# Sharing out projection chunks unevenly over the 32 attention items

## The reference, cut to what matters

```
proj = x @ w_in                       # queries, keys, values of four branches, and 4 x 1024 gates
y_c = moba_attention(...)             # "C": softmax
y_d = stick_breaking_attention(...)   # "D": see below
y_b = swa_sink_attention(...)         # "B": softmax in a window
y_a = dsa_attention(...)              # "A": softmax over the best 128 keys of an index score

# D, for each block of 128 queries:
z = q k^T * scale
log_keep  = where(strict, log_sigmoid(-z), 0)
log_after = reverse_cumsum(log_keep) - log_keep
a = where(strict, exp(log_sigmoid(z) + log_after), 0);  y = a v
```

## Time and profile before

| | |
|---|---|
| median of 3 runs | 1699.27 us (1697.19 to 1700.87) |
| the profiled execution | 1699.09 us, span 1697.4 us |
| PE busy | 1676.4 us (99% of the span) |
| DVE / ACT / POOL busy | 1225.5 / 779.0 / 818.4 us |
| granted TensorE clock, mean | 0.996 |
| the 32 items | from about 69 us to about 311 us |

### The profile page before, as it was taken

The page is one execution under the profiler, slowest core; times in us unless marked ns, Lnnn a source line. Parts: engine busy times, 40 slices in busy tenths (PEclk is TensorE's granted clock), DMA queues, the critical chain, the costliest instruction groups (busy, mean ns, idle before and its releaser), DMA issues.

```text
span 1697.4 us, 24495 instructions
## 1 busy us (share of the span) xinstructions
PE 1676.4 (99%) x9013; PEld 1483.0 (87%) x9013; DVE 1225.5 (72%) x2490; ACT 779.0 (46%) x1318; POOL 818.4 (48%) x493
## 2 busy tenths in 40 slices
PE   9999999999999999999999999999999999999997
PEld 7777777788889999999999999999888888888886
DVE  3588995512173985979988888435988888888886
ACT  4545545522334444773676477433333333333332
POOL 6332232444551667776866777775433233323312
PEclk9999999999999999999999999999999999999999
DMA  5121122243331566997899799997999999999952
GB/s 204 63 75 50 50 80 70 87 144 101 127 112 38 180 215 192 376 379 254 290 382 368 228 319 370 385 381 282 406 392 352 368 394 344 380 380 348 386 198 87
DMA packets 126502, 417.63 MB, mean 246 GB/s; under 512 B 12976, under 2 KB 32432, under 8 KB 124848
## 3 DMA queue, kind: packets, MB, share of 16 engines
q1 hardware_dynamic: 70320, 232.81, 39.1%
q0 software_dynamic: 36864, 134.23, 21.0%
q10 hardware_dynamic: 19200, 49.03, 7.3%
HBM read 364.91 MB, written 50.86 MB: 245 GB/s over the span
## 4 chain that ended last, share of the span: by engine, by line
PE 93%; DVE 3%; DMA 1%; POOL 1%; ACT 1%; issue 1%; SPq 0%; ACTq 0%; another core or an unknown queue 0%; DVEq 0%
PE ps L1365 18%; PE ps L1366 18%; PE ps L1367 17%; PE ps L1624 10%; PE ps L1627 10%; PE ps L1625 10%; PE ps L1735 5%; PE ps L1477 1%; PE ps L1429 1%; POOL w_lo L459 1%; PE ps L1460 1%; DMA raw<-w_units 1%; DMA x_raw<-xT 0%; PE ps L1406 0%; PE ps L1426 0%
## 5 line engine op out<-in xcount | busy, mean ns | idle before, releaser
L1365 PE MATMUL ps<-tok_hi,w_hi 128*128 128x384 f32 (+1 forms) x1472 | 526.4, 358 | 4.3 <-issue 4.3
L560 ACT ACTIVATE w_hi<-raw 128x1024 fp32r<-128x1024 f32 x330 | 348.9, 1058 | 389.3 <-PE ps L1627 291.3
L1367 PE MATMUL ps<-tok_hi,w_lo 128*128 128x384 f32 (+1 forms) x1472 | 517.4, 351 | 0.0
L1366 PE MATMUL ps<-tok_lo,w_hi 128*128 128x384 f32 (+1 forms) x1472 | 517.3, 351 | 0.0
L503 POOL TENSOR_TENSOR w_lo<-raw,w_hi 128x1024 fp32r<-128x1024 f32 x128 | 319.0, 2495 | 163.1 <-ACT w_hi L560 162.5
L459 POOL TENSOR_TENSOR w_lo<-raw,w_hi 128x1024 fp32r<-128x1024 f32 x76 | 183.4, 2416 | 319.7 <-ACT w_hi L560 319.5
L1365 PEld LDWEIGHTS ps<-tok_hi,w_hi 128*128 128x128 f32 x1472 | 276.7, 188 | 34.9 <-issue 15.2
L520 POOL DMA_INDIRECT v_got<-v_rows,eid x128 | 154.4, 1206 | 299.6 <-DVE own L1149 282.1
L1624 PE MATMUL ps<-w_hi,gh_hi 128*128 128x512 f32 x760 | 295.7, 389 | 0.0
L1625 PE MATMUL ps<-w_lo,gh_hi 128*128 128x512 f32 x760 | 295.7, 389 | 0.0
L1367 PEld LDWEIGHTS ps<-tok_hi,w_lo 128*128 128x128 f32 x1472 | 276.6, 188 | 18.1
(11 more groups left out here) (248 smaller groups left out, 1971.1 us busy)
## 6 DMA issues: line engine op xcount, KB each, us to landing
raw<-u_units SPq DMA_DIRECT2D x128, 512.0 KB
raw<-v_rows SPq DMA_DIRECT2D x128, 512.0 KB
raw<-w_units SPq DMA_DIRECT2D x78, 512.0 KB
gate_d<-stage ACTq DMA_DIRECT2D x12, 2048.0 KB
gelu_d<-gelu_t ACTq DMA_DIRECT2D x120, 192.0 KB
gelu_in<-gelu_d SPq DMA_DIRECT2D x30, 768.0 KB
gate_in<-gate_d SPq DMA_DIRECT2D x28, 768.0 KB
gate_in<-gate_d SPq DMA_DIRECT2D x2, 1536.0 KB
```

The source lines that it names most:

```text
L560: act.activation(hi_of(n), raw[:, n % RAW, :], ACT.Copy).then_inc(hi_done, 1)
L1365: pe.matmul(out_, l_hi, r_hi, start=start, stop=False)
L1366: pe.matmul(out_, l_hi, r_lo, start=False, stop=False)
L1367: return pe.matmul(out_, l_lo, r_hi, start=False, stop=stop)
```

## The change

Items 8 to 15 get shares of four, all others shares of three, in place of equal shares. The number of chunks in all (224) stays.

```
+D_SHARE, OTHER_SHARE = 4, 3
 ...
 def filled_by(s):
-    return 4 if s < -1 else KC + (KC * N_FILL - KC) * (s + 1) // N_ITEM
+    if s < -1:
+        return 4
+    shares = sum(D_SHARE if 8 <= i < 16 else OTHER_SHARE for i in range(s + 1))
+    return KC + (KC * N_FILL - KC) * shares // (8 * D_SHARE + 24 * OTHER_SHARE)
```

## The result

The changed kernel takes 1702.43 us in the median of 21 runs (1700.05 to 1708.87); the kernel before takes 1698.81 in 21 runs beside it (1697.19 to 1701.16). The ratio is 1.0022, 95% interval 1.0016 to 1.0028: 3.6 us slower; 1702.8 was forecast. The profiled execution took 1701.94, its span is 1700.2, its mean granted clock 0.997. In the changed file every line stands four lower: L1365 is now L1369, L1395 is L1399, L1426 is L1430, L572 is L576, L951 is L955.

The account below looks back on a forecast made before the run. PE, busy 99% of the span, was taken as the bound, so only its waits and clock count. Waits +2.1 and clock +1.45 on the profiled 1699.09, plus 0.18 to the median, gave 1702.8 us; range 1698.5 to 1706.

Parts of the forecast that it names:

- Item 6: Before unit 15, PE waits 3.55 us for ACT's value copy, which stands behind the exponentials of item 7 and one split.
- Item 7: Before unit 16, PE waits 0.9 us for ACT's value copy.
- Item 11: Before the weights, PE's present wait of 1.76 us for DVE's late `keep_lo` goes.
- Item 13: Before unit 22, PE waits 3.9 us for the value copy in place of 4.22; the covering chunks stand behind it.
- Items 14 and 15: Two POOL low parts in a row hold up DVE by up to 2.1 us more; extra chunks cover it, cost nothing.
- Item 24: In the B items PE closes in on DVE and waits 0.3 us for probabilities; bounds 0 and 1.5.
- Clock: Slow clock after the gap of item 6 costs 1.75 us; after item 13's it costs 2.05, 0.3 less than before.
- Sum: Over the whole kernel, waits of 8.65 less 6.57 give +2.1 us, clock +1.45, together +3.55: forecast 1702.8 us.
- 1 (the clock holds in item 6): All waits as forecast, but the 3.4 us gap in item 6 brings no slow clock: 1701.1 us; chance 24%.
- 2 (chunks cover item 13): PE reaches unit 22 no earlier than the copy, so that gap and its slow stretch go: 1696.5 us; chance 7%.
- 3 (DVE the bound in B): DVE becomes the bound in B and late D (items 14, 15, 24), adding 3.3 us: 1706.1 us; chance 12%.
- 4 (a shorter gap in item 6): ACT is free earlier, the gap in item 6 is shorter, nothing is felt: 1697.5 us; chance 4%.

Follow-up runs that it names:

- the run with the early copy: Changed kernel (four to three shares) with ACT's value copy moved ahead of the next item's exponents: 1695.02 us, ratio to before 0.9975.
- four to three shares and late low parts: Changed kernel with POOL held back in items 8 to 14 so low parts start later, value copy where it was: 1702.14 us, ratio 1.0013.
- equal shares with late low parts: Kernel before with POOL's low parts held back in items 8 to 14: 1691.59 us; with the value copy also moved ahead of the next item's exponents: 1690.68.
- the first items' shares alone: Kernel before with five chunks moved from items 0 to 7 into items 8 to 12, later items at 7: 1701.92 us, ratio 1.0013.
- the boundaries kept: Changed kernel, but items 0 to 6 keep 7 chunks and item 7 gets 2: 1700.33 us, ratio 1.0005.
- the gap filled: Changed kernel with 14 matmuls of unused result put into PE's gap in item 6: 1701.23 us, ratio 1.0012.
- equal shares with early copy: Kernel before (7 chunks an item) with ACT's value copy moved ahead of the next item's exponents: 1699.1 us, ratio 1.0.

## Why the prediction was right, step by step

- *Item 6*: right. 3.55 forecast, 3.58 measured, shown as 3.41. The copy that ends 0.1 ahead is the releaser, as the run with the early copy shows.
- *Item 7*: right. 0.9 forecast, 0.78 measured.
- *Item 11*: right. The 1.76 went.
- *Item 13*: the size came out, the reason only in part. I said 3.9, from a chain that is late by itself, "the same work when it arrives". Measured were 1.2 in item 12, which I had not named (the transposes of unit 20 wait for its read-out, behind the late chain), and 2.8 in item 13. The 2.8 are the floor above: the scores come later in PE's order, with two chunks between them and the boundary where there were five. I had used that very rule for item 6 and not asked it here. That 1.2 and 2.8 add up to about the 3.9 is luck. Before, the floor made only 0.3 of the wait (167.96 + 5.17 against 172.81, where PE was due), and the chain made the other 3.9 of the 4.22. The scores of the kernel before:

```profile
167.96 0.94 PE L1426 MATMUL ps<-projT 64*128 64x128 f32 x12
```

- *Items 14 and 15*: right. Two low parts in a row took 5.35 us and cost DVE some 2.1 and 2.2 (L955 took 2.51, the operation behind it 3.40 for 1.21 before), and no wait of PE followed. The cover is thin: with the copy early PE comes sooner and waits 0.9 in item 15.
- *Item 24*: mis-sized. 0.3 forecast, 0.6 and 0.2 shown, some 1.0 lost; within the bounds of 0 to 1.5.
- *Clock*: wrong in place, and too high in sum. Forecast 1.75 for item 6 and 2.05 for item 13; the profile has 2.75 and 0, so 2.75 for 3.8. A line drawn between a gap without a fall and one with a fall priced a thing that varies from run to run.
- *Sum*: the waits came to 9.4 for 8.65, the clock to 0.4 more than before for 1.45 more. The two errors offset each other; that the median lies within 0.4 us of the forecast is in part luck.
- *Rivals*: 1 (the clock holds in item 6) is not what the profiled execution did; how the other runs divide is not known. 2 (chunks cover item 13) fell; what would cover is the number of chunks between scores and boundary, and the change cuts it. 3 (DVE the bound in B) showed as 1.0 in item 24 and as nothing in items 14 and 15; it is this one, and not the last, that two blocked instructions in a row speak for. 4 (a shorter gap in item 6) fell: 3.58.

## What to carry to other kernels

Where one engine's work is filled in between two ends of another's chain, work out for each boundary that needs a release how long the release takes from the last thing the filling engine itself hands over, and how many pieces of fill stand in between; a new sharing moves that count at every boundary, not only where the shares grow. Before sharing out work differently to cover a late chain, look in the trace for what makes the chain late: here it was one DVE instruction an item held up by 2.1 us (mostly 2.5 in place of 0.42), and moving its neighbour brought 7 us where the new shares lost 3.6. A cure can show nothing in one kernel and bring 7 us in another: the early copy did nothing with equal shares and 7 with four to three, the late low parts the other way round. Try cures on both kernels, and in pairs.

## What the runs showed of the hardware that was not expected

The clock's answer to a gap is not the same from execution to execution. The kernel with four to three shares and late low parts has gaps of 3.42, 0.63 and 2.64 us in the one execution that was profiled, and its 12 runs go from 1697.8 us at a mean granted clock of 0.999 to 1704.2 at 0.995, with times rising as the clock sinks; the kernels of equal shares with late low parts, whose profiles have no such gaps, span about 1.5 us in five runs each. What decides whether a gap has a fall was not settled: the 2.64 us of item 13 had one where the gap of item 6 was filled and where the first boundaries were kept, and none in the changed kernel and in the one just named.

The price comes in two sizes. The profiles hold nine falls inside the items. Five began behind the gap, when PE was at work again; there the clock stayed at 0.50 for 3.4 us and 1.7 were lost (the first items' shares alone, item 6; the boundaries kept, items 12 and 13; the gap filled, item 13; four to three with late low parts, item 6). Four began inside the gap; there it stayed at 0.50 for 6.8 us, and half of what PE worked in it was lost: 2.4 (before, item 13), 2.75 (after, item 6), 3.0 (equal shares with early copy, item 15) and 3.1 (the first items' shares alone, item 13).
